# The feed-forward of a decoder step in seven block products instead of eight

## What is computed

```python
# x: (tokens, 1024)
h = rms_norm(x, norm_ffn_g) @ w_ff1        # 1024 -> 4096
x = x + square(maximum(h, 0)) @ w_ff2      # 4096 -> 1024
```

## Time and profile before

| | |
|---|---|
| median of 3 runs | 2802.61 us (2796.93 to 2806.55) |
| profiled execution, span from first to last instruction | 2792.8 us |
| profiled execution, its own time end to end | not given beside the span; the median of the runs lies 9.8 us above the span |
| TensorE busy | 2555.8 us (92%) |
| TensorE weight load busy | 2313.1 us (83%) |
| VectorE busy | 1143.4 us (41%) |
| ScalarE busy | 794.1 us (28%) |
| Pool busy | 257.6 us (9%) |
| traffic with DRAM | 165.28 MB read, 28.00 MB written |

### The profile page before, as it was taken

How to read it: one execution, slowest core, us unless ns; L and a number is a source line. 1 busy time by engine, 2 the same in 40 slices (tenths; PEclk the granted TensorE clock), 3 DMA queues, 4 the chain that set the end, 5 groups by cost and what they waited for, 6 DMA issues and landing times. The chain is left out here.

```text
span 2792.8 us, 48391 instructions
## 1 busy us (share of the span) xinstructions
PE 2555.8 (92%) x21166; PEld 2313.1 (83%) x21166; DVE 1143.4 (41%) x1977; ACT 794.1 (28%) x1267; POOL 257.6 (9%) x279
## 2 busy tenths in 40 slices
PE   5998799978996789996999999998899999999998
PEld 4996698847994455546999999986799999999998
DVE  4445666443335667634122324344442222222223
ACT  4324222211124344452121213114331222122211
POOL 1001333203102233310000000000000000000000
PEclk7997899978997999998999999999899999999999
DMA  8320100045121211265111115013011111111111
GB/s 295 103 78 21 18 4 4 4 158 113 49 62 48 73 46 61 76 231 194 46 46 46 46 46 149 9 46 129 23 38 47 53 46 46 46 46 46 46 46 70
DMA packets 179075, 192.05 MB, mean 69 GB/s; under 512 B 18230, under 2 KB 163041, under 8 KB 173768
## 3 DMA queue, kind: packets, MB, share of 16 engines
q1 hardware_dynamic: 168051, 124.97, 15.2%
q0 software_dynamic: 9888, 61.87, 6.2%
q10 hardware_dynamic: 926, 2.12, 0.2%
HBM read 165.28 MB, written 28.00 MB: 69 GB/s over the span
## 5 line engine op out<-in xcount | busy, mean ns | idle before, releaser
L3486 PE MATMUL ps<-ff_hidden_high,ff_high 128*128 128x352 f32 x768 | 247.7, 323 | 0.0
L3487 PE MATMUL ps<-ff_hidden_low,ff_high 128*128 128x352 f32 x768 | 246.6, 321 | 0.0
L3488 PE MATMUL ps<-ff_hidden_high,ff_low 128*128 128x352 f32 x768 | 246.4, 321 | 0.0
L451 PE MATMUL ps<-xf_h,ff_high 128*128 128x352 f32 x720 | 232.3, 323 | 2.1 <-DVE ff_low L440 2.1
L452 PE MATMUL ps<-xf_l,ff_high 128*128 128x352 f32 x720 | 230.8, 321 | 0.0
L453 PE MATMUL ps<-xf_h,ff_low 128*128 128x352 f32 x720 | 230.6, 320 | 0.0
L3086 PE MATMUL ps<-xn_h,me_gate_w_high 128*128 128x352 f32 x576 | 187.1, 325 | 5.1 <-DVE me_gate_w_low L3152 5.1
L3087 PE MATMUL ps<-xn_l,me_gate_w_high 128*128 128x352 f32 x576 | 185.8, 323 | 0.0
L3088 PE MATMUL ps<-xn_h,me_gate_w_low 128*128 128x352 f32 x576 | 185.5, 322 | 0.0
L3595 DVE TENSOR_TENSOR x<-x,ps 128x1056 f32<-128x1056 f32 x64 | 80.3, 1254 | 224.8 <-PE ps L3488 224.8
L3589 DVE TENSOR_TENSOR ff_hidden_low<-ff_act,ff_hidden_high 128x1056 fp32r<-128x1056 f32 x32 | 40.3, 1259 | 306.9 <-ACT ff_hidden_high L3561 306.9
(11 more groups left out here) (716 smaller groups left out, 6272.4 us busy)
## 6 DMA issues: line engine op xcount, KB each, us to landing
ff_raw<-in_w_ff SPq DMA_DIRECT2D x64, 512.0 KB, 4.0
me_gate_w_raw<-in_w_in SPq DMA_DIRECT2D x23, 512.0 KB, 3.9
pj_raw<-in_w_in SPq DMA_DIRECT2D x13, 512.0 KB, 4.6
xn_high<-xn_h POOLq DMA_DIRECT2D x1, 4224.0 KB, 14.5
xn_low<-xn_l POOLq DMA_DIRECT2D x1, 4224.0 KB, 25.4
xn_h<-xn_high POOLq DMA_DIRECT2D x1, 4224.0 KB, 16.7
xn_l<-xn_low POOLq DMA_DIRECT2D x1, 4224.0 KB, 26.8
xn_h<-xn_high SPq DMA_DIRECT2D x1, 4224.0 KB, 13.2
```

What stands on the lines that cost most here:

```text
L451: e.matmul(o, W.hi[:, z, k, :], rh[:, k, n], start=k == ks[0], stop=False)
L3486: e.matmul(o, W.hi[:, u % NSPL, 2 * k + z, :], hh[:, r, ns], start=k == 0, stop=False)
L3487: e.matmul(o, W.hi[:, u % NSPL, 2 * k + z, :], hl[:, r, ns], start=False, stop=False)
L3488: mm = e.matmul(o, W.lo[:, u % NSPL, 2 * k + z, :], hh[:, r, ns], start=False, stop=k == GB - 1)
```

## The change

The feed-forward is computed as a two-by-two block scheme with seven products instead of eight (Strassen's scheme in the form with shared sums), one level deep. The three dimensions of each product are halved: tokens into two sets of NH = 528, weights into A(0,0), A(0,1), A(1,0), A(1,1).

- A unit `u` is now 256 output channels from 1024 input channels, for all tokens: 7 products P1, P6, P2, P7, P5, P4, P3 in this order, each 4 blocks of weights x 2 halves of 264 columns x 3 parts. Units 0 to 15 are the up layer, 16 to 31 the down layer (4 groups of 4 units). Up and down are no longer interleaved: all up units run first.
- Sums of weights are made by Pool (`sums`), four of 128 x 512 elements a unit. Weight parts go through a ring of three products.
- Seven operands take the place of the activations: four blocks or sums that lie near, three sums that lie far. Before the up layer they are made from x: the parts of the first two thirds by Pool, the last third by VectorE. All seven are split by ScalarE and VectorE.
- In the up layer ScalarE copies P1 (`t1`) and does relu and square of one output; VectorE takes the other five products, squares three outputs and makes the sums of the four outputs (`hidden_sums`). SP stores 4 outputs and 3 sums to DRAM (`hid_dram`) for each unit.
- In the down layer SP reads each of 4 x 7 operands back (1056 KB, `stage`), through two buffers that lie where the outputs of the up layer lay; ScalarE and VectorE split them (`hidden_high`, `hidden_low`) after the products named in `hidden_after`. VectorE adds each product to `x` (`take_down`); P1 is collected over the four groups in four tiles of which three lie where the sums of the up layer lay.
- `stage_mem` no longer splits the first third and no longer makes the parts of a first weight block; the squares that it makes lie elsewhere.

The diff, cut to its core:

```diff
+NH = T // 2
+THIRD = T // 6
+HALVES = 3
+RINGW = 3
+NPAIR = 4 * D // P // 2
+NU = 2 * NPAIR
+P1, P6, P2, P7, P5, P4, P3 = range(7)
+KEPT = (0, 5, 1, 3, 4, 6, 2)
...
+def hidden_after(q):
+    out = []
+    for n in range(28):
+        g, i = divmod(n, 7)
+        at = 7 * (NPAIR + 4 * g - 1) + i + 2
+        if n in (1, 2):
+            at += n
+        if n in (3, 4, 5, 6):
+            at = 7 * NPAIR + n - 2
+        if at == q:
+            out.append(n)
+    return out
...
+    bank = lambda u, ab: flat[:, 1024 * ((3 * u + ab) % 4) + 512 - NH // 2:1024 * ((3 * u + ab) % 4) + 512 + NH // 2]
+    SLOT = {P1: 0, P2: 0, P6: 1, P7: 1, P4: 1, P5: 2, P3: 2}
+    PARTS = (slice(0, 2 * THIRD), slice(2 * THIRD, NH))
+    stage_of = lambda n: 0 if n < 3 else (n - 3) % 2
...
         @block.sync
+            def half(n):
+                v, b = divmod(n - HALVES, 2)
+                e.wait_ge(s_wl, 7 * v + (P7 if b == 0 else P4) + 1)
+                e.wait_ge(s_ws, 4 * v + 4)
+                e.dma_start(raw[:, n % HALVES, :, :], weight_half(K, u, j)).then_inc(s_in[n % HALVES], 16)
+            def store(u):
+                e.wait_ge(s_o, u + 1)
+                e.dma_start(kept[:, g, 0:4, k, :], outA[:, u % 2, :, :]).then_inc(s_sa[u % 2], 16)
+                e.dma_start(kept[:, g, 4:7, k, :], outB[:, :, :]).then_inc(s_sb, 16)
+            def stage(n):
+                if n == 0:
+                    e.wait_ge(s_sa[0], 16 * (NPAIR // 2))
+                elif n == 4:
+                    e.wait_ge(s_sa[1], 16 * (NPAIR // 2))
+                    e.wait_ge(s_sb, 16 * NPAIR)
+                elif n < 4:
+                    e.wait_ge(s_x2, n)
+                else:
+                    e.wait_ge(s_x2, n - 1)
+                e.dma_start(staged[stage_of(n)][:, :, :], kept[:, g, KEPT[i], :, :]).then_inc(s_st[stage_of(n)], 16)
+            for u in range(NU):
+                if 1 <= u <= NPAIR:
+                    store(u - 1)
+                if 2 * u + 3 < 2 * NU:
+                    half(2 * u + 3)
+                if 2 * u + 4 < 2 * NU:
+                    half(2 * u + 4)
+                if u == NPAIR - 1:
+                    for n in range(4):
+                        stage(n)
+                if u >= NPAIR:
+                    g, m = divmod(u - NPAIR, 4)
+                    if u == NPAIR:
+                        for n in range(4, 9):
+                            stage(n)
+                    elif m == 3 and g < 3:
+                        for n in range(7 * (g + 1) + 2, min(7 * (g + 2) + 2, 28)):
+                            stage(n)
...
         @block.gpsimd
+            def sums(u):
+                if u:
+                    e.wait_ge(s_wl, 7 * (u - 1) + P5 + 1)
+                e.tensor_tensor(tmp[0][:, :, :], A(u, 1, 0), A(u, 1, 1), ALU.add).then_inc(s_ws, 1)
+                e.tensor_tensor(tmp[1][:, :, :], tmp[0][:, :, :], A(u, 0, 0), ALU.subtract).then_inc(s_ws, 1)
+                e.tensor_tensor(A(u, 1, 0), A(u, 0, 0), A(u, 1, 0), ALU.subtract).then_inc(s_ws, 1)
+                if u:
+                    e.wait_ge(s_wl, 7 * (u - 1) + P3 + 1)
+                e.tensor_tensor(tmp[2][:, :, :], A(u, 0, 1), tmp[1][:, :, :], ALU.subtract).then_inc(s_ws, 1)
...
         @block.tensor
+            def product(q):
+                for z in range(2):
+                    cols = slice(NH // 2 * z, NH // 2 * z + NH // 2)
+                    for k in range(4):
+                        e.matmul(o[:, cols], wring[:, r, 0, k, :], high(i)[:, k, cols], ...)
+                        e.matmul(o[:, cols], wring[:, r, 0, k, :], low(i)[:, k, cols], ...)
+                        mm = e.matmul(o[:, cols], wring[:, r, 1, k, :], high(i)[:, k, cols], ...)
+            for q in range(NQ):
+                u, i = divmod(q, 7)
+                e.wait_ge(s_wl, q + 1)
+                if u == 0:
+                    e.wait_ge(s_x1, i + 1)
+                elif u >= NPAIR and (u - NPAIR) % 4 == 0:
+                    e.wait_ge(s_x2, 7 * ((u - NPAIR) // 4) + i + 1)
+                room(u, i)      # P2 after the take of P1, P7 of P6, P4 of P7, P3 of P5
+                product(q)
...
         @block.scalar
+            for q in range(NQ):
...
+                weights_high(q + RINGW)
+                for n in hidden_after(q):
+                    hidden_high(n)
...
         @block.vector
+            for q in range(NQ):
+                if q in rest:      # lows of the last four operands of the front
+                    operand_low(l, 0, a)
+                    operand_low(l, 1, b)
+                if u < NPAIR:
+                    take_up(u, i)
+                else:
+                    take_down(u, i)
+                weights_low(q + RINGW)
+                if u < NPAIR and i == P3:
+                    hidden_sums(u)
+                for n in hidden_after(q):
+                    hidden_low(n)
```

More of the change, by code:

```diff
@@ L3411, in _ @@
                 take(2, m)
[L3414 to L3449, removed]
@@ L3466, in _ @@
         @block.tensor
         def _(e):
[L3468 to L3473, removed]
-                ns = slice(NW * c, NW * c + NW)
-                for k in range(KD):
-                    e.matmul(K.ps[:, 3 * u + c, 0:NW], W.hi[:, u, k, :], xh[:, k, ns], start=k == 0, stop=False)
-                    e.matmul(K.ps[:, 3 * u + c, 0:NW], W.hi[:, u, k, :], xl[:, k, ns], start=False, stop=False)
-                    mm = e.matmul(K.ps[:, 3 * u + c, 0:NW], W.lo[:, u, k, :], xh[:, k, ns], start=False, stop=k == KD - 1)
-                return mm
@@ L3481, in down @@
[L3481 to L3485, removed]
-                        e.matmul(o, W.hi[:, u % NSPL, 2 * k + z, :], hh[:, r, ns], start=k == 0, stop=False)
-                        e.matmul(o, W.hi[:, u % NSPL, 2 * k + z, :], hl[:, r, ns], start=False, stop=False)
-                        mm = e.matmul(o, W.lo[:, u % NSPL, 2 * k + z, :], hh[:, r, ns], start=False, stop=k == GB - 1)
-                return mm
@@ L3493, in _ @@
             e.wait_ge(s_sq, 1)
             for k in range(KD):
-                mm = e.matmul(K.ps[:, 6, 0:T - LAST], K.c("ones"), xl32[:, k, end], start=k == 0, stop=k == KD - 1)
+                mm = e.matmul(K.ps[:, 6, 0:NL], K.c("ones"), squares[:, k, :], start=k == 0, stop=k == KD - 1)
             mm.then_inc(s_sum, 1)
-            e.wait_ge(W.s_lo, 2)
-            chunk(1, 0)
-            e.wait_ge(s_mid_l, 2)
-            chunk(0, 1)
-            chunk(1, 1)
-            e.wait_ge(s_xh, 1)
@@ new lines, in operand_high, with hidden_high @@
+            def operand_high(i, z):
+                e.activation(high(i)[:, :, PARTS[z]], whole(i)[:, :, PARTS[z]], ACT.Copy).then_inc(s_hA, 1)
+            def hidden_high(n):
+                g, i = divmod(n, 7)
+                b = stage_of(n)
+                e.wait_ge(s_st[b], 16 * (1 + sum(stage_of(l) == b for l in range(n))))
+                e.wait_ge(s_mm, 7 * (NPAIR + 4 * g - 1) + i + 1)
+                e.activation(high(i), staged[b][:, :, :], ACT.Copy).then_inc(s_xh2, 1)
+            e.activation(squares[:, :, :], x[:, :, end], ACT.Square).then_inc(s_sq, 1)
@@ new lines, in operand_low, with hidden_low @@
+            def operand_low(i, z, count):
+                c = PARTS[z]
+                e.wait_ge(s_hA, count)
+                mm = e.tensor_tensor(low(i)[:, :, c], whole(i)[:, :, c], high(i)[:, :, c].bitcast(F32), ALU.subtract)
+                if z:
+                    mm.then_inc(s_x1, 1)
+            def hidden_low(n):
+                e.wait_ge(s_xh2, n + 1)
+                i = n % 7
+                e.tensor_tensor(low(i), staged[stage_of(n)][:, :, :], high(i).bitcast(F32), ALU.subtract).then_inc(s_x2, 1)
@@ L3665, in _ @@
             e.wait_ge(s_o, NTI)
-            for m in range(ahead.nraw):
-                e.dma_start(ahead.raw[:, m, :, :], first(m).rearrange("(k p) n -> p k n", p=P)).then_inc(ahead.s_in[m], 16)
+            for n in range(HALVES):
+                e.dma_start(ahead.raw[:, n, :, :], weight_half(K, n // 2, n % 2)).then_inc(ahead.s_in[n], 16)
         @block.gpsimd
```

412 lines of the change are left out of this document (290 added, 122 removed).

## The result

The changed kernel is slower: 2823.98 us, median of 4 runs (2820.39 to 2825.01), beside 2799.77 us (2794.99 to 2806.55) for the kernel before on the same chip. The ratio is 1.0081, 95% interval 1.0064 to 1.0098. The forecast was 2819 us, slower with a chance of 0.58.

What follows compares the result with a forecast made beforehand. TensorE's matmul columns were taken as the bound. Products 654.3 + front 33 + first passage 40 + later passages 31 = 758.3 against 740.2; less 1.5, +16.6: span 2809.4, plus 9.8 carried over, 2819 us; range 2785 to 2850.

Steps and rivals of the forecast that it cites:

- The pace: Feed-forward matmuls of 264 columns: 121.7 ns each, 2.92 us a product, 654.3 us in all.
- Steady units hidden: Steady up and down units: added VectorE, ScalarE, Pool and transfer work is hidden behind TensorE and costs nothing.
- The rival in which Pool costs 42 us: All units: Pool's sums delay one product a unit by 1.3 us, 42 us on top, 2861; chance 0.15.
- The front: Stage start and first up unit: first product at about 25 us, 33 us lost, bounds 25 and 42.
- and some 3 more while VectorE reads the same memory: Front: Pool's last operand sum, due at 19.6 us, comes some 3 us later beside VectorE.
- The first passage: Last up unit into first down unit: operands return through two buffers, 40 us lost, bounds 25 and 55.
- it is issued at -8 and lands at -3: First passage: first operand's transfer, timed from the last up product's expected end, is issued at -8 and lands at -3.
- I count it within the bounds above: TensorE's clock after long stalls: up to 2.8 us more each, given no term of its own.
- The later passages: Three later operand changes in the down layer: 4.6 us an operand over two buffers, 3 x 10.5 = 31 us lost.
- The rival that the passages don't block: Passages: transfers land in 3.3 us, all stalls stay under 86 us, 2783 us; chance 0.22.
- The ends: Stage before 1 us sooner, last take behind the stage 0.5 us shorter: 1.5 us less together.
- The 9.8 us carried over: Profiled span to median of the runs: median taken as 9.8 us above the span, as before.

Runs made afterwards that it cites:

- experiment 2: Changed kernel with Pool making the sums of weights for unit 0 only, later units reusing them: 2819.87 us, ratio 1.0076 to the kernel before.
- experiment 3: Changed kernel with unit 16's first product collected in `t1`, and unit 15's store and operands 4 to 6 issued earlier by SP: 2814.84 us, ratio 1.0064.
- experiment 4: Changed kernel with only unit 16's first product collected in its own buffer, SP's order unchanged: 2816.25 us, ratio 1.0067.
- experiment 6: Changed kernel with down operands brought back and split in halves through four half buffers, store and collect orders unchanged: 2809.34 us, ratio 1.0034.
- Experiment 1: Changed kernel without bringing back operands of the second to fourth groups; all down products use the first group's: 2793.5 us, ratio 0.9989.
- experiment 5: Kernel of experiment 3 with down operands brought back and split in halves through four half buffers: 2796.35 us, ratio 0.9998.
- experiment 8: Kernel of experiment 5 plus the front's operand sums on VectorE and ScalarE taking up first-passage operand n behind product 110 + n: 2790.67 us, ratio 0.9960.
- experiment 9: Kernel of experiment 8 with the front's operand sums left on Pool: 2792.86 us, ratio 0.9990.
- experiment 10: Kernel of experiment 8 run once more unchanged, on one chip with experiment 9: 2790.51 us, ratio 0.9974.

## Why the prediction was right, and where its numbers were off

- **The pace** was right: 121.4 ns for 121.7. The Trainium skill's formula (TensorE: Matmul & The Clock Gate, Back-to-back issue gap), which the page gives for an isolated matmul, would have the products end 48 us sooner (an estimate from that page: 605 for 652.6); the trace does not agree with it for these fp32r matmuls.
- **Steady units hidden**: right. TensorE takes the bare pace in them, and only six up units lose 1.9 us together, which experiment 2 puts down to Pool. The rival in which Pool costs 42 us is out; Pool's share behind the first unit is 10.7 us by the traces of experiment 2, 8.8 of them in the passages.
- **The front** was right in its sum, 33.1 for 33, but by another path, so luck has a part in it. The forecast let the first product wait for Pool's last sum, "and some 3 more while VectorE reads the same memory". Pool's last sum ended 21.0 us after the stage's start (19.6 + 3 forecast) and was not waited for: ScalarE took it up 2.8 us later, since it had stood for VectorE's mean. The timeline of ScalarE:

```profile
2053.37 0.44 ACT L3693 ACTIVATE mm_rstd<-mm_rstd 128x288 f32<-128x288 f32 x1 [9.52 <-DVE mm_rstd L3829]
...
2058.79 1.36 ACT L3677 ACTIVATE ff_sums_high<-ff_sums 128x1408 fp32r<-128x1408 f32 x1
```

The path was VectorE's queue. There the forecast counted nothing for the work beside Pool (its 3 us stand on Pool's side), and it cost 8.0 us in three operations and 3.0 in the first four norms (5.11 us for what takes 2.07 a little earlier). Unit 0 lost 6.2, less than the 8, of which 2.8 are matmuls at the lower clock.

- **The first passage** is the mis-sized term: 50.2 us for 40, still within its bound of 55. The first step that failed is "it is issued at -8 and lands at -3". With 0 at 2375.92 + 20.39 = 2396.3, it was issued at -8.3 and landed 10.2 us later. The view of SP's transfers, 2384 to 2399, shows what was under way:

```profile
ff_staged<-hidden_operands SPq DMA_DIRECT2D x1, 1056.0 KB, 10.2
ff_raw<-in_w_ff SPq DMA_DIRECT2D x2, 512.0 KB, 8.2
hidden_operands<-ff_hidden_sums SPq DMA_DIRECT2D x1, 792.0 KB, 7.1
```

The forecast named the store and the halves and then gave the transfer the time that it has alone. At 0.33 MB a us the 2.9 MB of these four transfers are 8.7 us, and 10.4 with the 1.7 us that the forecast adds for landing. The chain is seen in the timelines of SP, ScalarE and VectorE:

```profile
2387.97 33.65 SPq L3540 DMA_DIRECT2D ff_staged<-hidden_operands  x4
...
2398.17 1.96 ACT L3684 ACTIVATE ff_operand_high<-ff_staged 128x2112 fp32r<-128x2112 f32 x1 [11.46 <-DMA ff_staged<-hidden_operands]
...
2400.17 2.36 DVE L3748 TENSOR_TENSOR ff_operand_low<-ff_staged,ff_operand_high 128x2112 fp32r<-128x2112 f32 x1 [12.73 <-ACT ff_operand_high L3684]
...
2402.45 0.70 DVE L3765 TENSOR_TENSOR ff_hidden<-ps,ff_first_product 128x528 f32<-128x528 f32 x1
...
2421.67 0.43 SPq L3526 DMA_DIRECT2D hidden_operands<-ff_hidden  x1
...
2432.64 0.71 DVE L3800 COPY ff_hidden_sums<-ps 128x528 f32<-128x528 f32 x1 [11.36 <-DMA hidden_operands<-ff_hidden_sums]
```

The low of the first operand ended at +6.2 (forecast 1.1), and P4 of unit 15 started right behind VectorE's take of P7, as forecast, but at +7.0. P2 of unit 16 waited for the store to +37.2 (forecast 30.7), P5 for its operand to +56.0 (47.4), and the unit ended at +70.6 (60).

So the slow transfer explains the first 5.2 us; the delay then grew to 6.5, 8.6 and 10.6. The second step that failed is the clock, "I count it within the bounds above": it was given no time. The stretches of TensorE for P4 of unit 15 and P2 of unit 16, us, busy, PEclk:

```profile
2403.29:2408.71 5.42, 5.42 (x25) 0.50 0.59 200
2433.49:2438.91 5.42, 5.42 (x25) 0.50 0.32 100
```

TensorE is busy all the time and takes 5.42 us for a product of 2.91. By the timelines the weight low of P4 is made behind P2 (2439.87 to 2441.03), and the next operand is issued behind that (2441.52), so the 2.5 us of P2 stand in the chain; P3 of unit 16, the last product, took 4.52. Of the 50.2 us some 40.8 are gaps between two matmuls and 9.5 are matmuls further apart than the pace. Otherwise each link is the one that the prediction names; experiments 3, 4 and 6 took links out, and 14.5, 9.0 and 9.6 us came back.

- **The later passages** were right: 32.9 for 31, four products ahead of need, a cycle of (2548.43 - 2523.88) / 5 = 4.9 us an operand, between the starts of six lows, for the 4.6 forecast. (The prediction's 3 x 10.5 is 31.5, which it takes as 31.) Experiment 1 shows that they are the whole loss of the down units behind unit 16, and experiments 5 and 6 that the round over two whole buffers was the bound of some third of them (9.9 and 12.7 of 32.9).
- **The rival that the passages don't block** fell with them: an operand landed in 4.8 us at best in the first passage, not in 3.3. What it asked, stalls of under 86 us, was met only when the passages were made shorter: the stages of experiments 8 to 10 are 1 to 8 us under the 739.9 of before.
- **The ends** were mis-sized by 1.2 us: the tail behind the stage grew by 0.7 instead of shrinking by 0.5.
- **From span to median.** The 9.8 us carried over were mostly chance. Where an execution has both, its time is about 2 us over its span (2825.01 and 2823.2 in the profiled one of after, 2.2 in those of before in experiment 10). So the profiled execution of before took some 2795 us, an estimate, as little as the lowest of its runs, while that of after was the highest of its four and its span lies only 0.8 under the median. Terms 13.8 us too low in the sum and a carry some 9 us too high left the forecast 5 us under the median. So the forecast is nearer than its working, by luck.

## What to carry to other kernels

Seven products for eight took 78.2 us of matmuls out of the stage (730.8 - 652.6) and raised its idle or slowed time from 9.4 us (740.2 - 730.8) to 118.3 (770.9 - 652.6): where a saving of arithmetic forces all activations of a layer to be kept and brought back, cost the rounds of the buffers and the queues behind them first, and then the columns. A transfer issued beside a burst of others is to be priced with their bytes in front of it, not by its time alone. Cut the pieces so that transfer and splitting overlap, and keep waits for stores out of the queue that frees the accumulators; here this was worth 30 us of the stage for the same bytes and the same arithmetic (experiment 5).

## What the runs showed of the hardware

- Beside Pool operations, VectorE operations that read two SBUF operands took up to five times as long: 2.82 and 3.63 us for the weight lows that take 0.69, 4.57 for a low that takes 1.62. Pool is slower too, and not only VectorE: a weight sum of 1.26 us, as it takes with VectorE idle at 2393, took 1.74 on average for the fourth of a unit. The timeline of Pool has one form of 1408 elements at two prices, where 1.63 us are VectorE's:

```profile
2041.20 3.17 POOL L3581 TENSOR_TENSOR ff_sums<-xf_scaled 128x1408 f32<-128x1408 f32 x1
...
2047.90 4.52 POOL L3584 TENSOR_TENSOR xf_scaled<-xf_scaled 128x1408 f32<-128x1408 f32 x1
```

- In the changed kernel the first matmul behind a stop of 5.6 us or more takes 0.56 us in the timeline, behind one of 1.0 to 2.7 us 0.36, where 0.28 is usual; in experiments 8 to 10 stops of 2.6 to 4.6 us have either. The granted clock of the 20 us around the longest stop was 0.57. A product behind a long stop took 5.42 us at 0.50, where 2.91 is usual. No run took the clock's part out by itself.
